# The first norm's root applied at the eviction of the mixer's projections, and six batches of roots in the tail

## The chip, the cores and the metric

The kernel runs on one core of one Trainium2 chip. The metric is device time of one execution in microseconds (us), the median of several runs. A core has TensorE (PE, matrix products), VectorE (DVE), ScalarE (ACT), GpSimd (POOL) and SyncE (SP, which issues most DMAs). Each engine takes its instructions in the order in which the program gives them and waits on semaphores.

## The reference, cut to what matters

One step of a hybrid encoder layer, for a prompt of 1024 tokens and 32 tokens of a running stream, D = 1024, everything fp32:

```python
def rms_norm(x, g):
    y = x * rsqrt(mean(x * x, -1) + EPS)
    return y * g
proj = rms_norm(x, norm_mix_g) @ w_in      # 8 projections of width 1024
lx, lg, q, k, v, rg, ga, gb = split(proj)
# RG-LRU branch: conv of width 4, two gates, a scan
xc = conv_b + sum(xp[:, j:j + L] * conv_w[j] for j in range(4))
r, i = sigmoid(xc_block @ lru_wa + ba), sigmoid(xc_block @ lru_wx + bx)
a = exp(-8 * r * softplus(-lambda)); mult = sqrt(1 - a * a)
h[t] = a[t] * h[t-1] + mult * i * xc
y_lru = (gelu(lg) * h) @ w_lru_o
# retention branch, 8 heads of 128: rotary q and k, chunkwise state, group norm
y_ret = (silu(rg) * head_group_norm(retention(rope(q), rope(k), v))) @ w_ret_o
out = x + (sigmoid(ga) * y_lru + sigmoid(gb) * y_ret) @ w_out
# then a top-1-group / top-2-expert mixture of 32 SwiGLU experts, a residual,
# and a final rms_norm of every row
```

The factor rsqrt(mean(x*x) + EPS) is one number per token, and g one per feature. So `(x * g) @ w` times the token's factor is the same projection as the norm's output times w.

## The kernel before, in words

Features lie on the partitions and tokens along the free dimension: T = 1056 tokens in CT = 3 columns of CW = 352. Every fp32 product is made of three fp32r products of a high and a low part: `w_hi`, `w_lo` for a block of 128 output features, `xn_hi`, `xn_lo` for the normalised x. A "product" is one block of 128 outputs for all tokens: 3 columns x 8 k x 3 matmuls.

`Mixer` holds two weight slots s = 0, 1, each with three PSUM banks, one per column. `Jobs` numbers the products of a slot (turn): SP loads the raw weights, POOL splits them (`split`), PE runs `column`, and an engine that empties a bank raises `tile_free[s]`, for which PE's next turn of the slot waits.

- `normalise` (L258): ACT squares x, PE sums over features with a matrix of ones, ACT takes the root, DVE the reciprocal and x * g * r per k, ACT makes `xn_hi`, DVE `xn_lo`. The first two products' columns run in between. DVE computes softplus of lambda in some 25 small steps while x lands.
- `lru` (L434), 8 blocks n: slot 0 holds the conv's input, slot 1 GELU's. ACT copies the first out of PSUM (`conv_input`, L522 to L529), applies GELU out of PSUM (L537), sigmoids (L544), exp and tanh (L551, L552), sqrt (L563). DVE runs `conv` (L576, L579), `mult` (L594 to L597) and `scan` (L604 to L615). PE's gate matmuls (L504), two per column, go between the columns of other products; their two banks `pg` are freed by the sigmoids of the column before. For blocks 0 and 1 they stand a column later than for the others.
- `merge` (L644), twice (`ml`, `mr`): u is split by ACT (L743) and DVE (L751), ACT takes the sigmoid of a gate product out of PSUM (L736), DVE multiplies it by the branch's product (L763).
- `retention` (L830), 8 heads, 7 of them in a loop: four products v, k, q, gate. ACT copies v, k and q out of PSUM and applies SiLU to the gate's (`take`, L1046; `srg` is the buffer). DVE rotates k (L1143 to L1146) and q (L1171 to L1180), accumulates the states (L1191 to L1197), masks scores (L1155), normalises and gates (L1133). PE turns tokens and features (L886, L888) and builds states (L968) in two further banks that follow one another in the fixed order of `Turns.ORDER`; ACT's `take_k_t` (L1079) empties the banks of turned k, the last of them right after the first SiLU.
- `experts`: 32 experts, PE-bound. In its tail (`last_step` of ACT, L2276 and L2290; DVE L2431 to L2442; POOL L2049) the rows of h are squared and summed, rooted in five batches (`BATCHES`), scaled and stored, and the last three experts' 96 rows each are scattered by six indirect DMAs.

The order on ACT within a block n of `lru` is what the prediction follows:

```python
for n in range(KD):
    sigmoids(n)
    decay(n)
    if n < LAST:
        conv_input(n + 1)
    act.wait_ge(m2_done, n + 1)
    act.activation(mu[:], mu[:], ACT.Sqrt).then_inc(mult_out, 1)
    if n < LAST:
        gelu(n + 1)
```

and on DVE: `mult(n)`, `conv(n + 1)`, `scan(n)`.

Of the kernel before, what the change touches and what calls it, by code (L numbers as in the profile page):

```python
# [85 lines left out]
CN_ID = 0  # L86
CN_TRI = CN_ID + P
# [4 lines left out]
CN_N = CN_SLOT + SLOTS  # L92
# [6 lines left out]
def shape_tables():  # L99
# [26 lines left out]
    cn[:, CN_ID:CN_ID + P] = np.eye(P)  # L126
# [40 lines left out]
class Mixer:  # L167

    def __init__(self, nc, ctx, R):
# [10 lines left out]
        self.spare = sb("spare", [P, T])  # L180
        self.psum = [self.bank_set(ctx, s) for s in range(2)]
# [76 lines left out]
def normalise(nc, keep, A, R, J, following):  # L258
# [6 lines left out]
    with ExitStack() as ctx:  # L265
        sb = lambda n, s, d=F32: ctx.enter_context(nc.sbuf_tensor(f"nm_{n}", s, d))
        sem = lambda n: R.spend(keep.enter_context(nc.semaphore(f"nm_{n}")))
        x = R.u.rearrange("p (c k t) -> p c k t", c=CT, k=KD)
        sq = [sb(f"square{b}", [P, KD, CW]) for b in range(2)]
        rms = [sb(f"rms{b}", [P, CW]) for b in range(2)]  # L270
        ones = sb("ones", [P, 4 * P])
        warm = sb("warm", [P, 2])
        sp_e, sp_s, sp_q, sp_a = (sb(n, [P, 8]) for n in ("sp_e", "sp_s", "sp_q", "sp_a"))
# [4 lines left out]
        sq_done, summed = sem("sq_done"), sem("summed")  # L278
        rms_done, xn_done = sem("rms_done"), sem("xn_done")
        hi_done, lo_done = sem("hi_done"), sem("lo_done")  # L280
        abs_done, exp_done = sem("abs_done"), sem("exp_done")
        lam_done, dve_step = sem("lam_done"), sem("dve_step")
        cols = lambda c: slice(c * CW, (c + 1) * CW)

    def sync(sp):
# [4 lines left out]
        sp.dma_start(R.par[:], A["par_columns"]).then_inc(par_in, 16)  # L290
        load(0)
        for s in range(2):
            J.load(sp, s, 0, following[s])
        load(1)
        load(2)
        sp.dma_start(R.const[:], A["const_small"]).then_inc(const_in, 16)
# [4 lines left out]
    def tensor(pe):  # L301
        def sums(c):
            if c == 2:
                pe.wait_ge(rms_done, 1)
            for m, ks in enumerate(PARTS[c]):
                pe.wait_ge(sq_done, PARTS_BEFORE[c] + m + 1)
                for k in range(ks.start, ks.stop):
                    mm = pe.matmul(total[c % 2][:, 0:CW], ones[:, 0:P], sq[c % 2][:, k, :],
                                   start=(k == 0), stop=(k == KD - 1))
            mm.then_inc(summed, 1)  # L310

        def column(s, c):
# [3 lines left out]
            for m, ks in enumerate(HALVES):  # L316
                pe.wait_ge(hi_done, 2 * c + m + 1)
# [3 lines left out]
            for m, ks in enumerate(HALVES):  # L321
                pe.wait_ge(lo_done, 2 * c + m + 1)
# [7 lines left out]
        sums(0)  # L330
        sums(1)
        for c in range(CT):
            for s in range(2):
                column(s, c)
                if c == 0 and s == 0:
                    sums(2)
        pe.wait_ge(const_in, 16)

    def scalar(act):
        def square(c):  # L340
            if c == 2:
                act.wait_ge(summed, 1)
            for m, ks in enumerate(PARTS[c]):
                act.wait_ge(x_in[c][m], 16)
                act.activation(sq[c % 2][:, ks, :], x[:, c, ks, :], ACT.Square).then_inc(sq_done, 1)

        def root(c):
            act.wait_ge(summed, c + 1)
# [12 lines left out]
        act.activation(sp_e[:], sp_a[:], ACT.Exp, scale=-1.0).then_inc(exp_done, 1)  # L361
        act.activation(warm[:, 1:2], R.eps[:], ACT.Sqrt)
# [4 lines left out]

        square(0)
        weights(0)
        root(0)  # L370
        weights(1)
        square(1)
        hi(0)
        root(1)
        square(2)
        hi(1)
        root(2)
        hi(2)
        act.wait_ge(par_in, 16)
        act.wait_ge(lam_done, 2)  # L380

    def vector(dve):
        dve.memset(ones[:], 1.0).then_inc(set_done, 1)
        dve.memset(R.eps[:], EPS).then_inc(set_done, 1)
        dve.memset(R.stage[:], 0.0)
        dve.wait_ge(par_in, 16)
# [3 lines left out]
        st.link(dve.tensor_scalar(sp_s[:], lam, -1.0, None, ALU.mult))  # L390
        dve.tensor_tensor(sp_a[:], sp_s[:], lam, ALU.max).then_inc(abs_done, 1)
        dve.wait_ge(exp_done, 1)
        st.link(dve.tensor_scalar(sp_q[:], sp_e[:], 2.0, None, ALU.add))
        st.link(dve.reciprocal(sp_q[:], sp_q[:]))
        st.link(dve.tensor_tensor(sp_e[:], sp_e[:], sp_q[:], ALU.mult))
        st.link(dve.tensor_tensor(sp_q[:], sp_e[:], sp_e[:], ALU.mult))
        st.link(dve.memset(sp_a[:], 1.0 / (2 * LOG_TERMS - 1)))
        for j in range(LOG_TERMS - 2, -1, -1):
            st.link(dve.tensor_tensor(sp_a[:], sp_a[:], sp_q[:], ALU.mult))
            st.link(dve.tensor_scalar(sp_a[:], sp_a[:], 1.0 / (2 * j + 1), None, ALU.add))  # L400
        st.link(dve.tensor_tensor(sp_a[:], sp_a[:], sp_e[:], ALU.mult))
        st.link(dve.tensor_scalar(sp_s[:], sp_s[:], 0.0, None, ALU.max))
        st.link(dve.scalar_tensor_tensor(out=sp_s[:], in0=sp_a[:], scalar=2.0, in1=sp_s[:],
                                         op0=ALU.mult, op1=ALU.add))
        dve.tensor_scalar(R.lam_neg[:], sp_s[:], -8.0, None, ALU.mult).then_inc(lam_done, 1)
        dve.tensor_scalar(R.lam_pos[:], sp_s[:], 8.0, None, ALU.mult).then_inc(lam_done, 1)
# [5 lines left out]

        weights(0)
        for c in range(CT):
            r = rms[c % 2]
            dve.wait_ge(rms_done, c + 1)
            st.link(dve.reciprocal(r[:], r[:]))
            for k in range(KD):
                ins = dve.scalar_tensor_tensor(out=x[:, c, k, :], in0=x[:, c, k, :],
                                               scalar=R.par[:, PR_GMIX + k:PR_GMIX + k + 1], in1=r[:],  # L420
                                               op0=ALU.mult, op1=ALU.mult)
                if k % 4 == 3:
                    ins.then_inc(xn_done, 1)
            for m, ks in enumerate(HALVES):
                dve.wait_ge(hi_done, 2 * c + m + 1)
                dve.tensor_tensor(M.xn_lo[:, ks, cols(c)], x[:, c, ks, :], M.xn_hi[:, ks, cols(c)].bitcast(F32),
                                  ALU.subtract).then_inc(lo_done, 1)
            if c == 0:
                weights(1)

    return Programs(sync, gpsimd, tensor, scalar, vector)


def lru(nc, keep, A, R, J, following):  # L434

    M = J.M
    with ExitStack() as ctx:
# [27 lines left out]
        xp_set = sem("xp_set")  # L465
        CG = XC // CT
# [51 lines left out]
    def scalar(act):  # L518
        def conv_input(n):
            if n:  # L520
                act.wait_ge(conv_step, n * CONV_STEPS)
            act.activation(xp[:, PAD + SEQ:PAD + SEQ + PAD],  # L522
                           R.par[:, PR_CACHE:PR_CACHE + 24].rearrange("p (j n) -> p j n", n=KD)[:, :, n], ACT.Copy)
            for c in range(CT):
                J.tile_ready(act, 0, n, c)
                lo, hi = c * CW, min((c + 1) * CW, SEQ)
                ins = act.activation(xp[:, PAD + lo:PAD + hi], psum[0][c][:, 0:hi - lo], ACT.Copy)
                if hi - lo < CW:
                    ins = act.activation(xp[:, PAD + S0:XP], psum[0][c][:, hi - lo:CW], ACT.Copy)  # L529
                ins.then_inc(M.tile_free[0], 1)  # L530

        def gelu(n):
            if n >= 2:
                act.wait_ge(u_done, n - 1)
            for c in range(CT):
# [11 lines left out]
        def decay(n):  # L547
            act.wait_ge(gate_free[0], n * CT + CT)
            if n >= 2:
# [4 lines left out]
        act.wait_ge(xp_set, 1)  # L554
        conv_input(0)
        gelu(0)
        for n in range(KD):
            sigmoids(n)
            decay(n)
            if n < LAST:  # L560
                conv_input(n + 1)
            act.wait_ge(m2_done, n + 1)
            act.activation(mu[:], mu[:], ACT.Sqrt).then_inc(mult_out, 1)  # L563
            if n < LAST:
                gelu(n + 1)

    def vector(dve):
# [32 lines left out]
        def scan(n):  # L600
# [12 lines left out]
            J.taken(dve, 1, n)  # L613
# [3 lines left out]
        dve.memset(xp[:], 0.0).then_inc(xp_set, 1)  # L617
        dve.wait_ge(xp_set, 1)
        conv(0)
        for n in range(KD):  # L620
            mult(n)
# [2064 lines left out]
```

## Time and profile before

| | |
|---|---|
| median of 3 runs | 1844.86 us (1843.6 to 1845.11) |
| profiled execution, its own time | 1845.6 us |
| its span in the trace | 1843.7 us |
| mean granted PE clock | 0.984 |

The page's slices (40 equal parts of the span, busy share in tenths; PEclk is the granted TensorE clock):

```profile
PE   8999999999999999999999979989999999999993
...
DVE  7565580001455445554621143367888888998886
ACT  5455460001122111221310023227878878788784
...
PEclk9999999999999999999999989989999999999997
```

A slice is 46 us. The start is in the first one, the RG-LRU blocks end in the sixth, the first merge in the tenth, retention in the twentieth, the second merge in the twenty-fourth; the experts begin in the twenty-seventh.

### The profile page before, as it was taken

How to read it: one execution, taken by the hardware profiler on the slowest of the kernel's cores; microseconds unless marked ns; L12 is line 12 of the kernel's file. 1: busy time of each engine (PE TensorE's matmuls, PEld its weight loads, DVE VectorE, ACT ScalarE, POOL GpSimd, SP SyncE). 2: the span in 40 equal slices, each digit the busy share in tenths (PEclk: the TensorE clock that was granted, in tenths of full speed). 3: DMA queues.
4: the chain of work that ended last, by engine and by line, in shares of the span. 5: the costliest groups of instructions: out<-in, count | busy, mean ns of one | idle time of the engine just before them, and what ended most of it. 6: DMA issues, size and time to landing. Idle time of an engine off the chain costs nothing. (4 is left out here: it accounts for less than half of the span.)

```text
span 1843.7 us, 25685 instructions
## 1 busy us (share of the span) xinstructions
PE 1781.3 (97%) x10105; PEld 1547.5 (84%) x10105; DVE 1063.2 (58%) x1242; ACT 780.6 (42%) x914; POOL 497.3 (27%) x286
## 2 busy tenths in 40 slices
PE   8999999999999999999999979989999999999993
PEld 6989999999999999999999978857777777777772
DVE  7565580001455445554621143367888888998886
ACT  5455460001122111221310023227878878788784
POOL 0432322223222222222233310022332332234331
PEclk9999999999999999999999989989999999999997
DMA  4111122223111111111132456558999999999993
GB/s 151 38 52 52 29 57 72 70 70 116 50 38 34 37 37 48 37 34 37 38 104 93 142 184 228 200 205 318 369 390 376 381 382 376 385 382 396 382 343 133
DMA packets 146514, 316.52 MB, mean 172 GB/s; under 512 B 11153, under 2 KB 106481, under 8 KB 121720
## 3 DMA queue, kind: packets, MB, share of 16 engines
q1 hardware_dynamic: 135896, 287.79, 42.4%
q0 software_dynamic: 10528, 27.48, 5.4%
q8 instruction: 63, 1.03, 0.2%
q14 instruction: 27, 0.22, 0.0%
HBM read 288.16 MB, written 36.47 MB: 176 GB/s over the span
## 5 line engine op out<-in xcount | busy, mean ns | idle before, releaser
L227 PE MATMUL job_ps<-xn_hi,w_hi 128*128 128x352 f32 x1488 | 494.0, 332 | 0.3 <-issue 0.3
L229 PE MATMUL job_ps<-xn_hi,w_lo 128*128 128x352 f32 x1488 | 478.3, 321 | 0.0
L228 PE MATMUL job_ps<-xn_lo,w_hi 128*128 128x352 f32 x1488 | 477.6, 321 | 0.0
L210 POOL CAST w_hi<-w_raw 128x1024 fp32r<-128x1024 f32 x78 | 85.3, 1094 | 765.5 <-issue 445.3
L227 PEld LDWEIGHTS job_ps<-xn_hi,w_hi 128*128 128x128 f32 x1488 | 279.4, 188 | 4.0 <-issue 0.7
L228 PEld LDWEIGHTS job_ps<-xn_lo,w_hi 128*128 128x128 f32 x1488 | 280.2, 188 | 2.3
L229 PEld LDWEIGHTS job_ps<-xn_hi,w_lo 128*128 128x128 f32 x1488 | 279.6, 188 | 0.0
L212 POOL TENSOR_TENSOR w_lo<-w_raw,w_hi 128x1024 fp32r<-128x1024 f32 x78 | 205.0, 2629 | 6.3
L2369 DVE TENSOR_TENSOR ex_raw_lo<-ex_raw,ex_w_hi 128x2048 fp32r<-128x2048 f32 x88 | 200.0, 2284 | 10.8 <-ACT ex_w_hi L2237 10.7
L2237 ACT ACTIVATE ex_w_hi<-ex_raw 128x2048 fp32r<-128x2048 f32 x88 | 168.8, 1918 | 52.8 <-PE ex_y L2106 23.9
L763 DVE TENSOR_TENSOR gate<-job_ps,gate 128x352 f32<-128x352 f32 x48 | 25.2, 525 | 280.0 <-PE job_ps L229 280.0
L736 ACT ACTIVATE gate<-job_ps 128x352 f32<-128x352 f32 x48 | 20.6, 463 | 276.0 <-DMA merged_lru<-gate 121.6
L2369 DVE TENSOR_TENSOR u_lo<-u,ex_w_hi 128x2048 fp32r<-128x2048 f32 x52 | 118.3, 2286 | 13.8 <-ACT ex_w_hi L2237 11.7
L2369 DVE TENSOR_TENSOR raw_more_lo<-raw_more,ex_w_hi 128x2048 fp32r<-128x2048 f32 x52 | 118.3, 2285 | 9.2 <-ACT ex_w_hi L2237 9.1
L2237 ACT ACTIVATE ex_w_hi<-u 128x2048 fp32r<-128x2048 f32 x52 | 99.5, 1917 | 35.3 <-PE ex_y L2106 14.7
L2237 ACT ACTIVATE ex_w_hi<-raw_more 128x2048 fp32r<-128x2048 f32 x52 | 99.6, 1917 | 28.6 <-PE ex_up L2106 12.3
L2104 PE MATMUL ex_gate<-ex_w_hi,ex_x_hi 128*96 128x512 f32 x260 | 103.9, 399 | 3.2 <-DVE ex_x_lo L2375 2.3
L2104 PE MATMUL ex_up<-ex_w_hi,ex_x_hi 128*96 128x512 f32 x260 | 104.3, 401 | 0.0
L2106 PE MATMUL ex_gate<-ex_w_hi,ex_x_lo 128*96 128x512 f32 x260 | 103.8, 399 | 0.0
L2106 PE MATMUL ex_up<-ex_w_hi,ex_x_lo 128*96 128x512 f32 x260 | 102.5, 394 | 0.0
L2015 POOL DMA_INDIRECT ex_rows<-xf_rows,h_row x32 | 91.5, 2859 | 36.6 <-POOL h_row L2003 23.7
L2104 PE MATMUL ex_y<-ex_w_hi,ex_h_hi 128*96 128x512 f32 x248 | 99.3, 401 | 0.0
(325 smaller groups left out, 3311.4 us busy)
## 6 DMA issues: line engine op xcount, KB each, us to landing
ex_raw<-in_w_chunks SPq DMA_DIRECT2D x88, 1024.0 KB, 10.2
u<-in_w_chunks SPq DMA_DIRECT2D x52, 1024.0 KB, 8.5
raw_more<-in_w_chunks SPq DMA_DIRECT2D x52, 1024.0 KB, 9.1
w_raw<-in_w_in SPq DMA_DIRECT2D x64, 512.0 KB, 4.1
merged_lru<-gate SPq DMA_DIRECT2D x8, 528.0 KB, 5.1
spare<-merged_lru SPq DMA_DIRECT2D x8, 528.0 KB, 5.8
merged<-gate SPq DMA_DIRECT2D x8, 528.0 KB, 4.9
w_raw<-in_w_lru_o SPq DMA_DIRECT2D x8, 512.0 KB, 4.2
```

Source lines behind the costliest of these rows:

```text
L210: pool.tensor_copy(M.w_hi[s][:], M.w_raw[s][:]).then_inc(M.hi_done[s], 1)
L212: pool.tensor_tensor(M.w_lo[s][:], M.w_raw[s][:], M.w_hi[s][:].bitcast(F32), ALU.subtract).then_inc(M.split_done[s], 1)
L227: pe.matmul(out, M.w_hi[s][:, k, :], x_hi[:, k, cols], start=(k == 0), stop=False)
L228: pe.matmul(out, M.w_hi[s][:, k, :], x_lo[:, k, cols], start=False, stop=False)
L229: mm = pe.matmul(out, M.w_lo[s][:, k, :], x_hi[:, k, cols], start=False, stop=(k == KD - 1))
L736: act.activation(sg[j % 2][:, c * CW:(c + 1) * CW], psum[s][c][:, 0:CW], ACT.Sigmoid).then_inc(M.tile_free[s], 1)
L763: dve.tensor_tensor(m[:, cols], psum[s][c][:, 0:CW], m[:, cols], ALU.mult).then_inc(M.tile_free[s], 1)
L2015: pool.indirect_dma_start(out=xe[b][0:SLOTS, :], out_offset=None, in_=xf_rows, in_offset=bass.IndirectOffsetOnAxis(ap=row[e % ROWS][:], ax ...
L2104: pe.matmul(out, a_hi, b_hi, start=first, stop=False)
L2106: return pe.matmul(out, a_lo, b_hi, start=False, stop=last)
L2237: act.activation(w_hi[n % SPLIT][:], raw[n % RAW], ACT.Copy).then_inc(hi_done, 1)
L2369: dve.tensor_tensor(w_lo[n % RAW], raw[n % RAW], w_hi[n % SPLIT][:].bitcast(F32), ALU.subtract).then_inc(lo_done, 1)
```

## The change: what it does

1. `start` takes the place of `normalise`. x * g (without the root) is split as it lands: ACT writes `xn_hi` with the weight g as scale, DVE `xn_lo` with one fused instruction per k. The squares are halved twice by DVE before PE sums them. The reciprocal root of each token is kept in `M.r` (128 partitions wide). SP loads the first weight block ahead of x.
2. Whoever needs a projection multiplies it by `M.r`: on DVE for the conv's input, GELU's input, the merge gates and the gate of retention. Their non-linear functions then run on ACT out of SBUF and in place. For q the factor is put once into the rotary tables; k gets it there and a second time, for v, by one more multiply per head.
3. Softplus of lambda moves behind the first conv.
4. The identity is a small input of its own; the other constants load in the second stage.
5. In the tail there are six batches of roots for five, two tiles' squares are taken earlier, and the third scatter to the sample rows goes ahead of the prompt's.

```diff
@@ start, scalar @@
+        weights(0)
+        hi(0)
+        weights(1)
         square(0)
...
+        hi(1)
+        square(1)
+        root(0)
+        hi(2)
+        square(2)
+        root(1)
         root(2)
@@ start, vector @@
         weights(0)
+        lo(0)
+        weights(1)
+        pairs(0)
+        lo(1)
+        pairs(1)
+        turned_round(0)
+        lo(2)
+        p.first_block(dve, 0)
+        pairs(2)
+        turned_round(1)
+        p.first_block(dve, 1)
+        turned_round(2)
+        p.first_block(dve, 2)
@@ lru, scalar @@
         def gelu(n):
-            if n >= 2:
-                act.wait_ge(u_done, n - 1)
-            for c in range(CT):
-                J.tile_ready(act, 1, n, c)
-                act.activation(gl[n % 2][:, c * CW:(c + 1) * CW], psum[1][c][:, 0:CW],
-                               ACT.Gelu_apprx_tanh).then_inc(M.tile_free[1], 1)
+            J.taken(act, 1, n)
+            act.activation(gl[n % 2][:], gl[n % 2][:], ACT.Gelu_apprx_tanh).then_inc(gelu_done, 1)
...
         gelu(0)
         for n in range(KD):
             sigmoids(n)
             decay(n)
-            if n < LAST:
-                conv_input(n + 1)
             act.wait_ge(m2_done, n + 1)
             act.activation(mu[:], mu[:], ACT.Sqrt).then_inc(mult_out, 1)
             if n < LAST:
                 gelu(n + 1)
+    def gate_input(dve, n, c):
+        if n >= 2 and c == 0:
+            dve.wait_ge(u_done, n - 1)
+        J.tile_ready(dve, 1, n, c)
+        at = slice(c * CW, (c + 1) * CW)
+        dve.tensor_tensor(gl[n % 2][:, at], psum[1][c][:, 0:CW], M.r[:, at], ALU.mult).then_inc(M.tile_free[1], 1)
@@ lru, vector @@
         conv(0)
+        softplus(dve)
         for n in range(KD):
+            if n:
+                for c in range(CT):
+                    gate_input(dve, n, c)
             mult(n)
             if n < LAST:
+                for c in range(CT):
+                    conv_input(dve, n + 1, c)
                 conv(n + 1)
             scan(n)
@@ merge, vector @@
     def vector(dve):
+        if not entry:
+            gate_input(dve, 0)
         u_lo_part(dve, before.late_k)
         for j in range(KD):
+            if j + 1 < KD:
+                gate_input(dve, j + 1)
@@ retention, scalar @@
-            take(1, h * 2 + 1, srg, ACT.Silu, lambda c: take_k_t(2) if c == 0 else None)
+            for c in range(CT):
+                J.tile_taken(act, 1, h * 2 + 1, c)
+                at = slice(c * CW, (c + 1) * CW)
+                act.activation(srg[:, at], srg[:, at], ACT.Silu).then_inc(silu_done, 1)
+                if c == 0:
+                    take_k_t(2)
@@ retention, vector: rotate (k only), then the loop behind q's rotation @@
-            ins = dve.tensor_tensor(x[:], x[:], half[:], ALU.add)
-            ins.then_inc(done, 1)
+            st.link(dve.tensor_tensor(x[:], x[:], half[:], ALU.add))
+            dve.tensor_tensor(x[:], x[:], M.r[:], ALU.mult).then_inc(done, 1)
...
             for c in range(3):
+                J.tile_ready(dve, 1, h * 2 + 1, c)
+                at = slice(c * CW, (c + 1) * CW)
+                dve.tensor_tensor(srg[:, at], psum[1][c][:, 0:CW], M.r[:, at], ALU.mult).then_inc(M.tile_free[1], 1)
                 bank, free = turns.ready(dve, kind, h, h, "kv", c)
@@ retention, vector, before the first head @@
+        for at in (TB_COS, TB_SIN):
+            dve.tensor_tensor(tb[:, at:at + T], tb[:, at:at + T], M.r[:], ALU.mult).then_inc(table_set, 1)
@@ retention, vector, last head @@
         p.next_split(dve, range(4))
+        p.next_gate(dve)
@@ experts, tail @@
-        BATCHES = ((0, 3), (3, 6), (6, NTILE + 1), (NTILE + 1, NTILE + 2), (NTILE + 2, NTILE + 3))
+        BATCHES = ((0, 2), (2, 4), (4, 7), (7, NTILE + 1), (NTILE + 1, NTILE + 2), (NTILE + 2, NTILE + 3))
...
             h_part(LAST - 1)
+            square_tile(0)
             hi(LAST - 1, 5)
+            act.activation(warm[:], R.eps[0:1, :], ACT.Sqrt)
             hi(LAST, 4)
-            act.activation(warm[:], R.eps[0:1, :], ACT.Sqrt)
+            square_tile(1)
             h_part(LAST)
             hi(LAST, 5)
```

## Rows read from the trace of the kernel before

**Rows 1.** The page, part 1 (totals) and part 5 (costliest groups; last columns busy and idle).
```profile
PE 1781.3 (97%) x10105; PEld 1547.5 (84%) x10105; DVE 1063.2 (58%) x1242; ACT 780.6 (42%) x914; POOL 497.3 (27%) x286
...
L763 DVE TENSOR_TENSOR gate<-job_ps,gate 128x352 f32<-128x352 f32 x48 | 25.2, 525 | 280.0 <-PE job_ps L229 280.0
```

**Rows 2.** Timeline of the start: start us, length us, engine, line, names, [idle before].
```profile
8.63 0.79 ACT L345 ACTIVATE nm_square<-u 128x704 f32<-128x704 f32 x1 [1.25 <-DMA u<-in_x_columns]
...
12.65 2.34 DVE L417 RECIPROCAL nm_rms<-nm_rms 128x352 f32<-128x352 f32 x1
...
15.03 4.06 DVE L419 SCALAR_TENSOR_TENSOR u<-u,par,nm_rms 128x352 f32<-128x352 f32 x8
...
19.00 3.15 DVE L426 TENSOR_TENSOR xn_lo<-u,xn_hi 128x1408 fp32r<-128x1408 f32 x2
...
51.08 0.40 PE L227 MATMUL job_ps<-xn_hi,w_hi 128*128 128x352 f32 x1 [0.28 <-issue]
```

**Rows 3.** Timeline of PE in the RG-LRU stage, gate matmuls.
```profile
121.28 1.35 PE L504 MATMUL lru_pg<-conv_out,w_gates 128*128 128x353 f32 x4
...
137.76 1.35 PE L504 MATMUL lru_pg<-conv_out,w_gates 128*128 128x353 f32 x4
...
142.79 1.35 PE L504 MATMUL lru_pg<-conv_out,w_gates 128*128 128x353 f32 x4
...
242.66 2.96 PE L504 MATMUL lru_pg<-conv_out,w_gates 128*128 128x353 f32 x8 [0.70 <-ACT r_gate L544]
```

**Rows 4.** Timeline of DVE in the RG-LRU stage.
```profile
86.07 2.29 DVE L606 TENSOR_TENSOR_SCAN hidden<-decay_a,i_gate 128x1024 f32<-128x1024 f32 x1
...
125.75 1.26 DVE L594 TENSOR_TENSOR mult<-decay_a 128x1059 f32<-128x1059 f32 x1 [9.23 <-ACT decay_a L551]
...
130.26 4.04 DVE L579 SCALAR_TENSOR_TENSOR conv_out<-conv_in,par,conv_out 128x1059 f32<-128x1059 f32 x3
...
136.50 4.35 DVE L606 TENSOR_TENSOR_SCAN hidden<-decay_a,i_gate 128x1024 f32<-128x1024 f32 x1
...
142.32 0.19 DVE L615 TENSOR_TENSOR u<-gelu_gate,hidden 128x32 f32<-128x32 f32 x1
```

**Rows 5.** Timeline of ACT in the RG-LRU stage.
```profile
124.54 1.18 ACT L551 ACTIVATE decay_a<-r_gate,lam_neg 128x1059 f32<-128x1059 f32 x1
...
134.62 1.28 ACT L544 ACT_TABLE_LOAD   x1
...
138.55 0.56 ACT L544 ACTIVATE r_gate<-lru_pg,par 128x353 f32<-128x353 f32 x1 [2.64 <-PE lru_pg L504]
```

**Rows 6.** Timeline of PE behind two gaps.
```profile
15.26 7.71 PE L308 MATMUL nm_total<-nm_square,nm_ones 128*128 128x352 f32 x16 [3.39 <-ACT nm_square L345]
...
111.17 1.43 PE L504 MATMUL lru_pg<-conv_out,w_gates 128*128 128x353 f32 x4 [2.96 <-issue]
```

**Rows 7.** Windows: stretch, busy time of each engine, granted clock PEclk, DMA share, GB/s.
```profile
20.00:22.00 2.00, 2.00 (x7) 1.21 (x6) 2.00 (x2) 0.50 (x1) 0.00 (x0) 0.81 0.36 94
```

**Rows 8.** Timeline of DVE, entry of the first merge.
```profile
261.99 12.48 DVE L751 TENSOR_TENSOR ml_u_lo<-u,ml_u_hi 128x1056 fp32r<-128x1056 f32 x8
```

**Rows 9.** Timeline of all engines, first head and one head of the retention loop.
```profile
454.82 1.25 DVE L1143 TENSOR_TENSOR ret_rotary_half<-ret_k_features,ret_tables 64x1056 f32<-64x1056 f32 x1 [12.43 <-DMA ret_state_in<-in_state_ret]
...
577.95 0.63 PE L886 MATMUL ret_turn<-const,ret_k_features 128*128 128x128 f32 x4 [0.26 <-DVE ret_k_features L1146]
...
589.41 0.34 ACT L1079 ACTIVATE ret_k_tokens<-ret_turn,ret_tables 32x128 f32<-32x128 f32 x1
...
592.34 1.05 PE L968 MATMUL ret_turn<-ret_v_tokens,ret_k_tokens 128*128 128x128 f32 x8
...
593.02 0.18 DVE L1180 TENSOR_TENSOR ret_q_features<-ret_q_features,ret_tables 128x32 f32<-128x32 f32 x1
```

**Rows 10.** Timeline of the tail, DVE and POOL.
```profile
1813.54 0.18 DVE L2438 RECIPROCAL ex_fi_rstd<-ex_fi_rms 128x3 f32<-128x3 f32 x1 [2.33 <-ACT ex_fi_rms L2290]
...
1827.95 1.27 POOL L2049 DMA_INDIRECT out<-ex_y_rows,rt_sample_row  x1 [33.91 <-DVE ex_y_rows L2442]
```

More of the change, by code:

```diff
@@ L302, in sums @@
         def sums(c):
+            pe.wait_ge(added, c + 1)
             if c == 2:
                 pe.wait_ge(rms_done, 1)
[L305 to L309, printed above, removed]
+            for k in range(2):
+                mm = pe.matmul(total[c % 2][:, 0:CW], ones[:, 0:P], sq[c % 2][:, k, :], start=(k == 0), stop=(k == 1))
             mm.then_inc(summed, 1)
@@ L329, in tensor @@
             pe.matmul(total[1][:], ones[:, 0:P], ones[:], start=True, stop=True)
-        sums(0)
-        sums(1)
         for c in range(CT):
[L333 to L336, printed above, removed]
+            column(0, c)
+            if c == 2:
+                sums(2)
+            column(1, c)
+            if c < 2:
+                sums(c)
         pe.wait_ge(const_in, 16)
@@ L389, in vector @@
         lam = R.par[:, PR_LAM:PR_LAM + 8]
[L390 to L406, printed above, removed]
+        st.link(dve.tensor_scalar(M.sp_s[:], lam, -1.0, None, ALU.mult))
+        dve.tensor_tensor(M.sp_a[:], M.sp_s[:], lam, ALU.max).then_inc(abs_done, 1)
         def weights(s):
@@ L431, in normalise, with lo @@
-    return Programs(sync, gpsimd, tensor, scalar, vector)
+        def lo(c):
+            for m, ks in enumerate(PARTS[c]):
+                dve.wait_ge(hi_done, PARTS_BEFORE[c] + m + 1)
+                for k in range(ks.start, ks.stop):
+                    ins = dve.scalar_tensor_tensor(out=M.xn_lo[:, k, cols(c)], in0=x[:, c, k, :], scalar=gain(k),
+                                                   in1=M.xn_hi[:, k, cols(c)].bitcast(F32), op0=ALU.mult, op1=ALU.subtract)
+                ins.then_inc(lo_done, 1)
@@ L565, in scalar, with first_block_begins, first_block, conv_input @@
                 gelu(n + 1)
+    def first_block_begins(dve):
+        dve.memset(xp[:], 0.0).then_inc(xp_set, 1)
+    def first_block(dve, c):
+        dve.wait_ge(M.r_done, c + 1)
+        conv_input(dve, 0, c)
+        gate_input(dve, 0, c)
+    def conv_input(dve, n, c):
+        if c == 0:
+            if n:
+                dve.wait_ge(conv_step, n * CONV_STEPS)
+                dve.wait_ge(xc_done, n)
+            else:
+                dve.wait_ge(xp_set, 1)
+            dve.tensor_copy(xp[:, PAD + SEQ:PAD + SEQ + PAD],
+                            R.par[:, PR_CACHE:PR_CACHE + 24].rearrange("p (j n) -> p j n", n=KD)[:, :, n])
+        J.tile_ready(dve, 0, n, c)
+        lo, hi, end = c * CW, min((c + 1) * CW, SEQ), (c + 1) * CW
+        ins = dve.tensor_tensor(xp[:, PAD + lo:PAD + hi], psum[0][c][:, 0:hi - lo], M.r[:, lo:hi], ALU.mult)
+        if hi < end:
+            ins = dve.tensor_tensor(xp[:, PAD + S0:XP], psum[0][c][:, hi - lo:CW], M.r[:, hi:end], ALU.mult)
+        ins.then_inc(M.tile_free[0], 1)
@@ L1306, in iota @@
         def iota(n, ts):
[L1308 removed]
+            return H.const[:, CN_IOTA:CN_IOTA + n].unsqueeze(1).broadcast_to((P, ts.stop - ts.start, n))
         st = Steps(None, step)
```

248 lines of the change are left out of this document (131 added, 117 removed).

## The prediction

> **What bounds the kernel now.** I read the page's totals first: TensorE (PE) is busy 97% of 1843.7 us, VectorE (DVE) 58%, ScalarE (ACT) 42% [rows 1]. PE takes its instructions in one order, so the time is PE's work plus every wait in that order, and a delay of any PE instruction before the tail moves the end one for one. The timelines of the changed stages then show three places where the other engines' order matters: the start, the eight RG-LRU blocks, the retention heads; the tail is the fourth. I count against the profiled execution's own 1845.6 us, 0.7 above the median of the runs shown. A difference of 0.2% (3.7 us) is about what a measurement of this kernel can tell from no change.
>
> **The start.** PE's first ordinary product begins at 51.08 [rows 2]. Before it, each third of x waits for its root, a reciprocal (2.34) and eight scalings (4.06) on DVE before it can be split. Afterwards the split doesn't wait for the root. I follow DVE, the longest chain. The first third of x lands at 8.63 [rows 2], now behind one 512 KB weight block: about 10.1 (estimate). ACT's last pair 0.8, DVE's last pair 1.1 (0.51 each, a fused instruction of 352 columns): 12.1. Second weight split 14.0; the squares on ACT end at 15.9 (four of 0.79), pair sums 2.5 (the 1408-column subtraction takes 1.57, half of 3.15, and half that again): 18.4. Then second third 4.1, its pair sums 2.5, reciprocal 2.3, third third 4.1, first block's two evictions 1.1, pair sums 2.5: 35.0. PE now waits there for the sums: 1.2, and 3.9 for the last column: 40.1 instead of 51.08. The conv of block 0 waits for two more reciprocals and the last evictions and comes some 1.1 later than PE asks. Gain 9.8, bounds 7 and 11. The logarithm's some 25 small operations move behind that conv and end before the first decay asks for them: nothing.
>
> **The RG-LRU blocks.** This is the term that decides. Times from here are offsets from PE's last gate matmuls of a block (121.28 [rows 3]).
> Before: the three multiplies of `mult` start at +4.47 and the conv's three accumulating ones at +8.98 [rows 4], one short instruction (0.86) earlier the conv itself, +8.1. The scan part ends at +21.2 (142.51). Meanwhile PE has a product and a column to do: it asks for gate matmuls (n+1, 0) at +16.48 and (n+1, 1) at +21.51 [rows 3]. For these ACT is ready: GELU of the next block has run long before, and the sigmoid's table is loaded at 134.62, before the sigmoids at 138.55 [rows 5]. DVE is idle 9.2 before the next `mult` [rows 4].
> After: ACT's order is still GELU(n+1), sigmoids(n+1), but GELU now waits for `gate_input(n+1)`, which stands on DVE behind `scan(n)`. And PE's gate matmuls (n+1, 1) reuse a bank that sigmoid (n+1, 0) must empty. So what was parallel becomes one loop: mult, conv input, conv, scan, gate input, GELU, table load, sigmoid, PE, mult.
> Its length: `conv_input` on DVE is three multiplies out of PSUM, 0.525 each [rows 1], overlapping, with a small copy 1.7. That moves conv and scan from an end of +21.2 to +22.9 with every duration kept. The scan of 1024 columns is 4.35 beside POOL's split and 2.29 in a block where none runs [rows 4]; being later it misses part of it, while the conv takes some on: I take +21.9. Gate input 1.5: +23.4. GELU over 1056 columns out of SBUF, near the 1.18 of the exponential: +24.6. The sigmoid's table load, hidden before, 1.28 [rows 5]: +25.9. First sigmoid 0.56: +26.4. PE asked at +21.51: a wait of 4.9 in each of blocks 3 to 6. Block 1 the same, 5.0. In block 2 PE asks at +20.8 (its first gates come at 111.17 after their own wait of 2.96, and the column order changes there), so 5.7. In block 7 three gate steps stand back to back, ending at 245.62, +18.2 from block 6's last gates (a block repeats after 16.48 + 2 x 5.03 = 26.54, four times from 121.28 is 227.4) [rows 3]; now the first sigmoids are at +26.4 to +27.0 and two more rounds follow: +29.4, so 11.2. Sum 5.0 + 5.7 + 4 x 4.9 + 11.2 = 41.5. Bounds: POOL beside the scan as before, 1.0 more a block, 48; everything on DVE at its fastest, 1.0 less, 34.
> The Trainium skill, "ScalarE: Activation LUTs", section "What ACT_TABLE_LOAD costs", puts a switch at about 2.66 us with its drain. Here the exponential starts right behind a load of 1.28, so the row decides; by the page the loop would be 1.4 longer, some 9 us more in all.
>
> **PE's clock.** After a 3.39 us gap PE's matmuls begin at 15.26 and sixteen of them take 7.71; the granted clock is 0.81 of full from 20 to 22, so half (1.2 GHz) until about 20.7: 5.4 us [rows 6, 7]. After a gap of 2.96 the gate matmuls take their usual time (1.43 against 1.35) [rows 3, 6], so that gap cost no clock. The new gaps of 4.9 lie beyond both. A half-rate stretch of 5.4 costs 2.7 of work, all of it between gates (n+1, 1) and (n+1, 2), which is inside the loop. I take 2.4 for each of seven gaps, 16.8; bounds 0 and 20. The Trainium skill, "TensorE: Matmul & The Clock Gate", section "HAM oscillation — how this bites in real kernels", says that a kernel whose waits recur pays the return to full rate at every one of them. The trace bears it out once in two such gaps.
>
> **Merges.** Each gate tile is multiplied on DVE (1.5) and then goes through the sigmoid, a product ahead of its use: nothing in the steady part, PE's 11.5 us product covers it. At the entry of the first one `gate_input(0)` stands before the eight subtractions that start at 261.99 and take 1.56 each [rows 8]; PE uses the sixth about when it is done. Plus 1.2 there, and 1.5 at the second merge, where it stands before the last head's gating. Bounds 0 and 2 each. If the cover were gone in the steady part it would be 1.5 for each of 14, 21.
>
> **Retention.** Two waits, both seven times. (a) The rotated k gets one more multiply of 1056 columns, 1.26 (the first of the rotation takes 1.25). PE already waits 0.26 for the rotated k at 577.95 [rows 9], so all of it lands on PE: 1.3. Beside POOL's split it could be 3.3. (b) `srg` is now filled by DVE after the q rotation, which ends at 593.20, later 594.5. Column 0's multiply 0.5, ACT's SiLU 0.6 with its signals, and only then ACT empties the last k bank (0.34, which it did at 589.41): 595.9. PE's state matmuls of column 1 need that bank; they ran at 592.34, shifted by (a) 593.6 [rows 9]. Wait 2.3. Together 3.6 by 7 = 25.2. Bounds: 1.3 by 7 = 9 if (b) is covered, 5 by 7 = 35. First head: the two tables are scaled once, DVE stands waiting for them already (12.43 for the DMA [rows 9]), so 2.6 more. I count no clock in gaps of 2.3; if it fell each time, 2 by 7 = 14.
> q's rotation, later by the same, costs nothing further: its scores are asked for some 4 us behind it.
>
> **Tail.** DVE waits 2.33 for the second root at 1813.54 [rows 10]. With smaller batches and two squares moved ahead it finds work there; against that the last weight splits come 0.9 later, since ACT squares a tile (0.9 beyond its own idle time) in between. 2.33 + 0.18 (a reciprocal that stood there) - 0.9 = 1.6. POOL's six scatters, which start at 1827.95, come that much earlier; the third sample scatter, moved up, finds its rows just ready. Gain 1.6, bounds 0 and 2.4.
>
> The constants (256 KB) load in the second stage, some 100 us before their use: nothing.
>
> **Sum.** -9.8 + 41.5 + 16.8 + 1.2 + 1.5 + 25.2 + 2.6 - 1.6 = +77.4. 1845.6 + 77.4 = 1923.0.
>
> **Rivals.**
> 1. The loop closes but PE keeps its full clock: 1923.0 - 16.8 = 1906. For it, the 2.96 gap; against it, the 3.39 one. Chance 0.22; forecast with the clock 0.52.
> 2. Half rate after retention's gaps as well (14), the first k multiply contended: 1923 + 14 + 8 (1.2 more a head) = 1945. The gaps of 2.3 are shorter than one that kept the clock. 0.10.
> 3. The loop doesn't close: gate input and GELU run in DVE's and ACT's idle time as they do now (DVE is idle 9.2 a block), and retention alone pays: 1845.6 - 9.8 + 2.7 + 27.8 - 1.6 = 1865. Against it stands the order of the code: every link is an explicit wait. 0.08.
> 4. The other side, faster: the same, and PE also finds cover in retention, since ACT's and DVE's half-idle time takes the moved work. Then the start and the tail are left: 1845.6 - 9.8 - 1.6 = 1834. It decides if the moved chain in a head stays under 0.3 and in a block under 3.5 (PE's slack: conv ready at +13, asked for at +16.5). 0.07.
> The last 0.01 is no change.
>
> **How the numbers follow.** The likeliest is 1923. Low end 1886: loop at its lower bound (34), no clock, retention at 2.5 a head, the start at its best. High end 1948: case 2 and a little. That leaves out cases 3 and 4 and the extremes. Faster by over 0.2% 0.07, within 0.01, slower 0.92.
>
> **What would show it.** PE's first ordinary product at about 40. The starts of `mult` some 33 to 34 apart instead of 26.5, with PE waiting 5 for a sigmoid before each block's second gate matmuls, and a granted clock under 1 in that stage. Heads 62.2 apart instead of 58.6, PE waiting for ACT's k tokens. The end of all PE work some 79 later. It is wrong if PE has no wait at those gate matmuls: then GELU wasn't behind the scan.

## The result, and the profile after

The changed kernel takes 1924.09 us (median of 4 runs, 1921.64 to 1928.62), the kernel before 1844.61 beside it: 1.0429 times as long, 95% interval 1.0417 to 1.0442. The profiled execution took 1921.95 with a span of 1920.1, 76.4 more than before. The forecast was 1923.0.

The page's totals, and of its slices the rows that answer to those of before (a slice is now 48 us):

```profile
PE 1792.5 (93%) x10069; PEld 1554.8 (81%) x10069; DVE 1129.4 (59%) x1389; ACT 772.5 (40%) x876; POOL 486.5 (25%) x286
...
PE   8887869999999999999999997998999999999994
...
PEclk9998989999999999999999998998999999999997
```

PE falls from 97% to 93% [rows 1], and the missing tenths stand in the first six slices; in the fourth and the sixth PEclk dips too. The view of waits says for whom PE waited (engine and line that waits, releaser: us in total, times, the longest), after the change:

```profile
PE lru_pg L505 <- ACT r_gate L528: 39.8, 7, 10.4
PE ret_turn L1019 <- ACT ret_k_tokens L1130: 14.2, 7, 2.1
PE ret_turn L937 <- DVE ret_k_features L1199: 12.4, 8, 1.6
PE op_out L1712 <- DVE op_m_lo L1807: 11.1, 1, 11.1
PE lru_pg L505 <- issue: 6.7, 3, 4.0
```

The same waits before it:

```profile
PE lru_pg L504 <- issue: 3.2, 2, 3.0
PE ret_turn L886 <- DVE ret_k_features L1146: 1.8, 7, 0.3
PE lru_pg L504 <- ACT r_gate L544: 0.7, 1, 0.7
```

The first of the five is the loop that the forecast saw in the RG-LRU blocks, the next two are its waits (b) and (a) in retention. The fourth was there (10.8). The fifth, waits of a block's first gates for the conv, was 3.2 in total.

PE's timeline (start, duration, engine, line, count, idle before), which answers to [rows 3] for blocks 2 to 4 and 7. With the loop closed, a wait of 5.5 stands before each block's second gates; from there to the third gates it is 7.50 and 7.26, where it was 5.03:

```profile
126.17 1.35 PE L505 MATMUL lru_pg<-conv_out,w_gates 128*128 128x353 f32 x4
142.65 1.35 PE L505 MATMUL lru_pg<-conv_out,w_gates 128*128 128x353 f32 x4
153.37 2.72 PE L505 MATMUL lru_pg<-conv_out,w_gates 128*128 128x353 f32 x4 [5.53 <-ACT r_gate L528]
160.87 1.35 PE L505 MATMUL lru_pg<-conv_out,w_gates 128*128 128x353 f32 x4
177.34 1.35 PE L505 MATMUL lru_pg<-conv_out,w_gates 128*128 128x353 f32 x4
188.07 2.72 PE L505 MATMUL lru_pg<-conv_out,w_gates 128*128 128x353 f32 x4 [5.54 <-ACT r_gate L528]
195.33 1.35 PE L505 MATMUL lru_pg<-conv_out,w_gates 128*128 128x353 f32 x4
...
290.98 4.58 PE L505 MATMUL lru_pg<-conv_out,w_gates 128*128 128x353 f32 x8 [10.41 <-ACT r_gate L528]
```

The loop itself, on DVE (first fence) and ACT (second), read from one `mult` to the next; it answers to [rows 4, 5]:

```profile
130.64 1.26 DVE L626 TENSOR_TENSOR mult<-decay_a 128x1059 f32<-128x1059 f32 x1 [14.19 <-ACT decay_a L537]
...
134.36 1.34 DVE L568 TENSOR_TENSOR conv_in<-job_ps,rstd 128x352 f32<-128x352 f32 x3
...
136.71 4.69 DVE L611 SCALAR_TENSOR_TENSOR conv_out<-conv_in,par,conv_out 128x1059 f32<-128x1059 f32 x3
141.32 2.34 DVE L617 COPY stage<-conv_in 128x3 f32<-128x3 f32 x1
...
145.09 2.29 DVE L638 TENSOR_TENSOR_SCAN hidden<-decay_a,i_gate 128x1024 f32<-128x1024 f32 x1
...
148.95 1.38 DVE L578 TENSOR_TENSOR gelu_gate<-job_ps,rstd 128x352 f32<-128x352 f32 x3
165.34 1.26 DVE L626 TENSOR_TENSOR mult<-decay_a 128x1059 f32<-128x1059 f32 x1 [15.00 <-ACT decay_a L537]
```

```profile
150.37 1.08 ACT L522 ACTIVATE gelu_gate<-gelu_gate 128x1056 f32<-128x1056 f32 x1 [13.57 <-DVE gelu_gate L578]
151.47 1.28 ACT L528 ACT_TABLE_LOAD   x1
152.76 0.56 ACT L528 ACTIVATE r_gate<-lru_pg,par 128x353 f32<-128x353 f32 x1
```

DVE now idles 14 to 15 us a block and ACT 13.0 to 13.6 at its longest wait: each waits for the other or for PE's next gates. `mult` starts 34.2 to 34.7 apart in blocks 3 to 6 instead of 26.5; the forecast had 33 to 34.

The ledger: each row is the difference of one and the same instruction's start (in the RG-LRU row its end) in both traces, less that of the row above. The entry of a merge is DVE's first product of an output column and its gate.

| stage | forecast | measured |
|---|---|---|
| start (first gates, 58.79 to 49.35) | -9.8 | -9.4 |
| RG-LRU (last gates' end, 245.62 to 295.56) | 41.5 + 16.8 = 58.3 | 59.4 |
| entry of the first merge (278.17 to 328.64) | +1.2 | +0.5 |
| first head (first turned k on ACT, 464.76 to 516.89) | +2.6 | +1.7 |
| retention, second merge's entry (931.25 to 1011.93) | 25.2 + 1.5 = 26.7 | 28.6 |
| second merge, experts (last matmul, 1812.72 to 1892.40) | 0 | -1.0 |
| tail (to the end of the span) | -1.6 | -3.3 |
| sum (the rows are rounded) | +77.4 | +76.4 |

### The profile page after: what moved, and what is told of

Same layout as the page of the kernel before. It is cut to its first block and busy times, and to the rows that moved or that the text cites. A ratio compares the mean times of both kernels' runs of the same rounds, so it can differ in the third digit from the quotient of the medians.

```text
span 1920.1 us, 25758 instructions
## 1 busy us (share of the span) xinstructions
PE 1792.5 (93%) x10069; PEld 1554.8 (81%) x10069; DVE 1129.4 (59%) x1389; ACT 772.5 (40%) x876; POOL 486.5 (25%) x286
## 3 DMA queue, kind: packets, MB, share of 16 engines
q8 instruction: 63, 1.03, 0.2%
## 5 line engine op out<-in xcount | busy, mean ns | idle before, releaser
L229 PE MATMUL job_ps<-xn_hi,w_hi 128*128 128x352 f32 x1488 | 500.4, 336 | 0.0
L229 PEld LDWEIGHTS job_ps<-xn_hi,w_hi 128*128 128x128 f32 x1488 | 283.8, 191 | 4.5 <-issue 1.7
L230 PEld LDWEIGHTS job_ps<-xn_lo,w_hi 128*128 128x128 f32 x1488 | 284.1, 191 | 3.2 <-issue 1.5
L773 ACT ACTIVATE gate<-gate 128x352 f32<-128x352 f32 x48 | 22.5, 497 | 257.1 <-DVE gate L796 257.0
L811 DVE TENSOR_TENSOR gate<-job_ps,gate 128x352 f32<-128x352 f32 x48 | 25.2, 524 | 144.9 <-PE job_ps L231 144.9
```

The lines of the kernel that those rows point to most:

```text
L229: pe.matmul(out, M.w_hi[s][:, k, :], x_hi[:, k, cols], start=(k == 0), stop=False)
L230: pe.matmul(out, M.w_hi[s][:, k, :], x_lo[:, k, cols], start=False, stop=False)
```

## The experiments

"Blocks" is the time from the first gates to the end of the last ones in the trace: 186.8 before, 246.2 after.

### Gate input ahead of the scan

```diff
-            if n:
-                for c in range(CT):
-                    gate_input(dve, n, c)
             mult(n)
...
                 conv(n + 1)
+                for c in range(CT):
+                    gate_input(dve, n + 1, c)
             scan(n)
```

> The changed kernel with gate_input(n+1) on VectorE moved from behind scan(n) to between conv(n+1) and scan(n). ScalarE's order is untouched: GELU(n+1) still stands ahead of the sigmoids. Theory: the 59.3 us that the RG-LRU blocks lost are the loop through scan, gate input, GELU, table load and sigmoid; with gate input ready at about 16.5 behind a block's last gates, the sigmoids are ready at 20, ahead of TensorE's 21.5, and waits and clock loss both go: mult starts 26.5 apart again, time 1924.1 - 59 = 1865, 1861 to 1870. Rival: the blocks are longer because VectorE has 3.2 us more work in each (conv input and gate input) or because ScalarE's order alone is at fault: then moving one step on VectorE changes little, time above 1900.

Measured 1879.65 (ratio to before 1.0181, 1.0164 to 1.0198): 44.4 less than the changed kernel, 15 above the expected 1865 and outside its range. Blocks took 201.0. The mechanism holds, since the waits for sigmoids fell from 39.8 in seven to 6.0 in five, but the opening was too small. ACT's GELU started at 160.25, 18.9 behind the last gates, where I had gate input ready at 16.5: a copy of three elements ahead of gate input takes 2.35 here too. PE still waits 0.23 in blocks 3 to 6, and in block 7, whose gate steps stand back to back, 5.10.

### GELU later on ScalarE

```diff
-        gelu(0)
         for n in range(KD):
             sigmoids(n)
             decay(n)
+            gelu(n)
             act.wait_ge(m2_done, n + 1)
             act.activation(mu[:], mu[:], ACT.Sqrt).then_inc(mult_out, 1)
-            if n < LAST:
-                gelu(n + 1)
```

> The changed kernel with GELU(n) on ScalarE moved from ahead of the sigmoids of its block to between tanh and the square root. VectorE's order is untouched, gate input stays behind the scan; as many table loads as before. Theory: this opens the same loop at another link, so it gives the same as the kernel with gate input moved: about 1865, 1861 to 1870. Rival: it is the position of gate input on VectorE that delays mult or frees TensorE's banks too late; then the waits stay, time above 1900.

Measured 1874.95 (1.0166, 1.0136 to 1.0195; runs from 1869.36 to 1879.76). No wait for a sigmoid is left in its trace:

```profile
133.27 1.35 PE L505 MATMUL lru_pg<-conv_out,w_gates 128*128 128x353 f32 x4
138.30 1.35 PE L505 MATMUL lru_pg<-conv_out,w_gates 128*128 128x353 f32 x4
143.33 1.35 PE L505 MATMUL lru_pg<-conv_out,w_gates 128*128 128x353 f32 x4
159.80 1.35 PE L505 MATMUL lru_pg<-conv_out,w_gates 128*128 128x353 f32 x4
```

26.53 a block, as before, with DVE's order untouched: the rivals of the two runs, which blamed gate input's place on DVE or DVE's added work, fall. Two links of one loop were cut by independent edits, and both opened it. But blocks take 194.4, 7.6 more than before; the expectation left that out, and the median lies above its range. Of the time, 49 came back. The executions are up to 10 apart; only one of them has a trace, so why is not shown, and the run with the k bank below has a likely reason.

### The gap filled

```diff
+        def unused(n, c):
+            if c == 1 and n >= 3:
+                pe.wait_ge(M.tile_free[0], (n + 1) * CT)
+                for _ in range(28):
+                    pe.matmul(M.psum[0][2][:, 0:CW], M.w_hi[0][:, 0, :], M.xn_hi[:, 0, 0:CW], start=True, stop=True)
...
-                J.product(pe, 0, n + 1, M.xn_hi, M.xn_lo, lambda c: gates(n, c))
+                J.product(pe, 0, n + 1, M.xn_hi, M.xn_lo, lambda c: (unused(n, c), gates(n, c)))
```

> The changed kernel with the loop left as it is; in blocks 3 to 6 TensorE runs 28 unused matmuls of 352 columns (0.16 us each, 4.5 us) in the gap of 5.5 us before the second gate matmuls; nothing waits for them. Theory: the column behind the gap runs at half rate because of the gap (gates 2 to gates 3 take 7.0 to 7.5 instead of 5.03), and with the gap filled they take 5.0: four times 2.0 to 2.4 less, 1924.1 - 8.8 = 1915. Rival: the column is slow for another reason (missing operands, a bank, ports): nothing changes, 1924.

Second to third gates now take 5.16, four times (151.71 to 156.87 for one), and blocks 237.9, 8.3 less where 8.8 was expected. In windows behind block 3's second gates (us, busy time and count of the five engines, PEclk, DMA share, GB/s), the changed kernel and then this one:

```profile
153.00:158.00 5.00, 4.63 (x12) 3.63 (x13) 0.00 (x0) 1.88 (x4) 0.00 (x0) 0.50 0.00 0
```

```profile
151.00:156.00 5.00, 4.29 (x23) 3.86 (x24) 0.00 (x0) 2.21 (x5) 0.00 (x0) 1.00 0.01 3
```

The granted clock is 0.50, that is 1.2 GHz, behind a gap of 5.5 and full, 2.4 GHz, behind one of 1.0, in the same place with the same operands. The gap is the cause of the slow column. The time agrees less well: 1918.76 (1.0397, 1.0380 to 1.0414) where 1915 was expected, three runs at 1918.7 to 1919.0 and the profiled one at 1912.56, 9.4 under the changed kernel's profiled one. Where the other three lost 6 us has no trace.

### The k bank emptied ahead of SiLU

```diff
+            take_k_t(2)
             for c in range(CT):
                 J.tile_taken(act, 1, h * 2 + 1, c)
                 ... ACT.Silu
-                if c == 0:
-                    take_k_t(2)
```

> The changed kernel with ScalarE emptying the last bank of turned k ahead of the gate's SiLU in retention, so not behind VectorE's q rotation. Theory: TensorE's 2.1 us wait for the k tokens goes in each of seven heads, and nothing takes its place: 1924.1 - 14.7 = 1909; heads 60.1 apart, and 58.6 + 1.4 for the wait on the rotated k is what is left. If the two heads that took 1.6 longer did so for a clock that fell behind this wait, 3 more: 1906. Rival: the wait moves to the scores or to the next product's bank, since SiLU and q's rotation stay late: less than 5 us gained.

Measured 1903.29 (1.0315, 1.0298 to 1.0332), 20.8 less, and less than either expectation (1909, or 1906 with the clock). The wait for the k tokens is gone and the other stays:

```profile
PE ret_turn L937 <- DVE ret_k_features L1198: 12.4, 8, 1.6
PE ret_turn L937 <- ACT ret_k_tokens L1130: 1.0, 1, 1.0
```

Behind the first head the heads are 59.9 apart, all six distances: 2.26 less, 15.8 over seven waits. The rest comes from the clock. In the changed kernel four of the six distances are near 62.2 and two are 63.7, one of them here:

```profile
696.97 0.63 PE L937 MATMUL ret_turn<-ident,ret_k_features 128*128 128x128 f32 x4 [1.59 <-DVE ret_k_features L1199]
760.71 0.63 PE L937 MATMUL ret_turn<-ident,ret_k_features 128*128 128x128 f32 x4 [1.59 <-DVE ret_k_features L1199]
822.87 0.63 PE L937 MATMUL ret_turn<-ident,ret_k_features 128*128 128x128 f32 x4 [1.59 <-DVE ret_k_features L1199]
```

In the traces of the five other kernels with this wait one to three of the six are long. Two by 1.6 and 15.8 make 19.0; the profiled executions differ by 18.6. The changed kernel's windows in that long head, PE's k-bank wait of 2.06 standing at 711.5 to 713.56:

```profile
708.00:713.00 5.00, 3.50 (x22) 3.21 (x21) 4.63 (x8) 0.33 (x1) 0.00 (x0) 1.00 0.27 81
713.00:718.00 5.00, 4.44 (x21) 4.47 (x22) 2.93 (x8) 0.91 (x3) 0.00 (x0) 0.68 0.00 0
718.00:723.00 5.00, 5.00 (x33) 4.66 (x32) 1.56 (x3) 0.50 (x1) 2.66 (x2) 0.98 0.00 0
```

So a gap of 2.0 to 2.1 took the clock in some heads and not in others, at 1.6 each. How many heads it hits varies from trace to trace. That this also spreads the executions of one kernel is likely and not shown, since each kernel has one trace: with the wait gone the four runs lie within 1.8, and the 6.2 between the two groups of the run with the filled gap would be four more long heads.

### Tables of their own for k

```diff
+        tk = M.gate
...
-            st.link(dve.tensor_tensor(x[:], x[:], half[:], ALU.add))
-            dve.tensor_tensor(x[:], x[:], M.r[:], ALU.mult).then_inc(done, 1)
+            dve.tensor_tensor(x[:], x[:], half[:], ALU.add).then_inc(done, 1)
...
+        for i, at in enumerate((TB_COS, TB_SIN)):
+            dve.tensor_tensor(tk[i][:], tb[:, at:at + T], M.r[:], ALU.mult).then_inc(table_set, 1)
```

> The changed kernel with rotary tables of their own for k, which hold the square of the root's factor (written once, into the merge's two gate buffers), so that the multiply of 1056 columns behind each head's k rotation goes. Theory: of TensorE's 1.5 to 1.6 us wait for the rotated k, 1.3 go in each of seven heads, and the first head pays two more table multiplies less its own k multiply, 1.3: 1924.1 - 9.1 + 1.3 = 1916. The wait for the k tokens stays 2.1, since q's rotation moves with k's. Rival: the wait for the rotated k is hidden or the k tokens' wait grows by as much: 1924, with the first head's cost 1925.

Measured 1914.64 (1.0376, 1.0360 to 1.0391), 9.5 less, the theory's 8 and a little. Five of the six distances between heads are 60.86 instead of 62.15, 1.3 less each, and one is 62.43. The first head pays with a wait of 3.5 instead of 1.3. The wait for the k tokens stayed 14.2 in total.

### The tail alone

The change's edits of `BATCHES`, the squares, `turned_round` and POOL's scatters, put into the kernel before.

> The kernel before with the edits of the tail alone: six batches of roots, two squares moved ahead, the third scatter to the sample rows moved up. The forecast had 1.6 us for them; between the two traces the distance from TensorE's last matmul to the end of the span shrinks by 3.2 us. Theory one: 1.6, so 1843.7 where the kernel before takes 1845.3. Theory two: 3.2, 1842.1. Rival: the scatters wait for stores that come no earlier, 1845.3.

Measured 1842.66 against 1845.85: ratio 0.9982, 0.9973 to 0.9991, over 11 runs. 3.2, not 1.6. DVE in the tail of the kernel before and in this one:

```profile
1809.68 0.18 DVE L2438 RECIPROCAL ex_fi_rstd<-ex_fi_rms 128x3 f32<-128x3 f32 x1 [1.03 <-ACT ex_fi_rms L2290]
```

```profile
1808.91 1.40 DVE L2432 SCALAR_TENSOR_TENSOR ex_rows<-ex_y,h_w_slot,ex_rows 96x512 f32<-96x512 f32 x2
1810.23 0.15 DVE L2439 RECIPROCAL ex_fi_rstd<-ex_fi_rms 128x2 f32<-128x2 f32 x1
1810.42 2.47 DVE L2443 SCALAR_TENSOR_TENSOR ex_raw<-ex_raw,ex_fi_rstd,ex_fi_g 32x1024 f32<-32x1024 f32 x2
```

DVE waited for two roots, 1.03 and 2.33 [rows 10], 3.4 together; now it waits for neither. POOL's first scatter goes from 1827.95 to 1825.32, 2.6 earlier, and a pause of 0.57 among the scatters is 0.30 now, so the last of them ends 2.9 earlier.

### The conv's input ahead of mult

```diff
             if n < LAST:
                 for c in range(CT):
                     conv_input(dve, n + 1, c)
-                conv(n + 1)
+            mult(n)
+            if n < LAST:
+                conv(n + 1)
```

> The kernel with the late GELU, and with conv_input(n+1) on VectorE moved from behind mult(n) to ahead of it, where VectorE is idle. In the trace of the late GELU alone the eight blocks still take 7.6 us more than before (194.4 against 186.8): TensorE waits 4.0 instead of 2.96 for conv of block 2 and 2.5 instead of 0.3 for that of block 7, with a half-rate stretch behind the first. Theory: the conv input behind mult makes every conv 1 to 2 us late, and both waits and the half-rate stretch come from that; moved ahead, 7 less than the late GELU alone: 1875 - 7 = 1868, blocks in 187.5. Rival: the conv is late because of contention or because mult starts later: no change, 1875.

Blocks 187.8, as the theory had it: the waits for the conv fell from 4.0 to 2.95 and from 2.50 to 0.30. But the time is 1871.33 (1.0137, 1.0122 to 1.0153), only 3.6 less than with the late GELU alone where 7 was expected; as the two intervals overlap, the times alone do not show a gain. A new wait of 3.7 in total for `ml_u_lo` stands at the first merge's entry. DVE reaches its subtractions too late for a PE that comes 6.6 us sooner.

### All four together

> The late GELU, the early conv input, the k bank emptied ahead of SiLU, and the tables for k, all together. Theory: what is left of the change is its gain at the start (9.4) and in the tail (3.2 by the traces), against 0.5 at the first merge, some 5 for the first head's tables and 1.5 at the second merge: 1845.3 - 12.6 + 7 = 1840, 1834 to 1844; heads 58.6 apart, blocks 26.54 apart, granted clock 0.98 or more. Rival: the four losses hide one another, so that a further wait (scores, GELU, the gate's bank) comes up once they are gone: above 1850.

Measured 1846.53 against 1845.85 (1.0008, 0.9999 to 1.0017): 6.5 above the theory and outside its range, not as far as the rival's 1850, but of its kind: no difference from before. The four losses are gone (blocks 186.3, heads 58.6), and further waits came up, at two entries, where the start's gain is lost again:

```profile
PE ret_turn L937 <- DVE ret_k_features L1197: 5.2, 8, 3.1
PE job_ps L229 <- DVE ml_u_lo L785: 3.7, 2, 2.6
```

The windows behind both (us, PE busy and count, PEclk, DMA share, GB/s):

```profile
265.00:270.00 5.00, 4.88 (x22) 0.71 0.36 105
...
465.00:470.00 5.00, 5.00 (x21) 0.57 0.36 105
```

PE's last gates end 9.8 earlier than before, the first merged column is 4.1 earlier (274.03), the first turned k 0.1 earlier (464.62), and PE's last matmul starts 1.5 later (1814.26). Only the tail's gain brings the time back to that of before.

### The entries mended

The kernel of the section before with these further edits:

```diff
+            if n < LAST:
+                gelu(n)
             act.wait_ge(m2_done, n + 1)
             act.activation(mu[:], mu[:], ACT.Sqrt).then_inc(mult_out, 1)
...
+        gelu(LAST)
...
+            else:                                    # block 7, behind mult(n)
+                for c in range(CT):
+                    gate_input(dve, n, c)
...
+                early = KD - 2 if entry else 4       # k 0 to 3 of all columns first
+                for ks in (range(early), range(early, KD)):
...
+        dve.tensor_tensor(tk[1][:], M.r[:], M.r[:], ALU.mult).then_inc(table_set, 1)
+        dve.wait_ge(table_set, 1)
         dve.wait_ge(table_in, 32)
...
             rotate(st, k_f, 1, h * 2, k_rot)
+            if kind == "first":
+                for at in (TB_COS, TB_SIN):          # q's tables, now behind k's rotation
...
```

> The kernel with all four losses mended, with three more edits where its trace shows the start's gain lost again: in block 7 gate input stands behind mult and GELU behind the root (VectorE idles 1.2 there); the first merge's first output product runs k 0 to 3 for all three columns and then 4 to 7, so that it asks later for the low parts; in retention the squared root is formed before the tables land, and q's tables are scaled behind the first k rotation. Theory: in that trace TensorE waits 1.2 and 2.6 at the first merge's entry with a half-rate stretch behind (1.9), and 3.1 for the first rotated k with another (2.2); some 2.5 and 1.9 of the first group go and 3 and 2 of the second, 9 in all less what the last low parts still cost (1.5): 1846.5 - 8 = 1838.5, and a few us faster than the kernel before. Rival: the waits are set by the DMA of the tables and by the scan of block 7, not by VectorE's order: less than 3 gained, 1844 or more, no difference from before.

Measured 1834.48 (1833.62 to 1836.02) against 1846.14: 0.9939, 0.9925 to 0.9953. It beats the kernel before by 11.7 and the changed one by 89.6 us, and is 4 better than expected. The wait for `ml_u_lo` is gone and that for the first rotated k too; what is left of the latter's line is 0.3 a head:

```profile
PE lru_pg L505 <- issue: 3.2, 2, 3.0
...
PE ret_turn L943 <- DVE ret_k_features L1203: 2.1, 7, 0.3
```

Of the 11.7, 3.2 are the tail's by its own run; the other 8.5 are by subtraction what is left of the start's 9.4. The trace agrees: PE's last matmul starts at 1804.65, 8.1 earlier than before. The edits of the two entries ran together only, so which of them removed how much is not shown.

## Why the prediction was right

The start: 9.4 of 9.8; PE's first ordinary product began at 41.18, said 40. The loop in the blocks closed as described, and each of two single edits opened it; retention's two waits came as described, and one edit removed each. The single terms:

- Waits for sigmoids, forecast 5.0, 5.7, four times 4.9 and 11.2; measured 4.42, 2.85, four times 5.5 and 10.41, 39.8 for 41.5. Block 2 was over-estimated because I held its first gates' own wait at 2.96; the conv's later input raised it to 4.04, and block 7's from 0.29 to 2.50. These 3.5 us were not in the sum. They more than made up for waits that were 1.7 smaller; two errors met, and that their signs differ is luck.
- Within the loop, the step "being later it misses part of it, while the conv takes some on: I take +21.9" was wrong in its parts. The scan fell all the way to 2.29, which gives 2.06 back, and a three-element copy rose from 0.16 to 2.34. The conv took on 0.65 (4.04 to 4.69), and the multiply ahead of the scan gave 0.69 back (1.95 to 1.26). Gate input started at +22.8 and not +21.9, hence 5.5 and not 4.9.
- Clock, forecast 16.8. In blocks 3 to 6 it is 2.5, 2.2, 2.1, 2.0 between second and third gates. Over the stage 16.8 is what is left when 39.1 more wait for sigmoids and 3.5 more for the conv are taken from 59.4; that all of it is clock is not shown. Rival 1, full clock, is refuted by PEclk 0.50 behind the gap and by the filled gap. That a gap of 2.96 kept the clock in the one trace I had was luck of that execution: after 2.95 with the conv's input early, the next gates came 6.67 later, with the entries mended 6.68, with all four edits 5.09.
- Retention, forecast 3.6 a head. (a) was 1.3, as the run with tables shows. (b) was 2.0 to 2.1, forecast 2.3; undoing it gave 2.26. I counted no clock; 3.2 came of it in the profiled execution, so rival 2 held in two heads. The entry of the second merge took some 0.8 and not 1.5 (from the last head's rotated k to it 63.15 instead of 60.30, less the 2.01 of wait (b)). Over the stage that is 28.6 for 26.7.
- The tail is the term that was mis-sized most in proportion, 1.6 for 3.2: "2.33 + 0.18 - 0.9 = 1.6". Of the 0.9 of late weight splits at most 0.3 shows (PE's last matmul at 1813.06 with the tail alone, 1812.72 before), and a first wait of 1.03 was missed.
- Experts: 1.0 came back, where PE's longest waits for `ex_x_lo` and for the gathered rows went from 2.3 and 1.5 to 1.3 and 1.0. This wasn't tried further.
- The low end, 1886, is not what its own terms give: 1923 less 7.5 for the loop, 16.8 for the clock, 7.7 for retention and 1.2 for the start is 1890. And a table load that is 1.4 longer in seven blocks would cost near 10 more, where the forecast says some 9. Nothing in the outcome hangs on either.

Rival 3, no loop, and rival 4, cover in retention, fell with the first trace.

## What to carry to other kernels

A value that moves from one engine to another keeps its old place in the second engine's program unless you move that too: the projection's scaling went to VectorE behind the scan, while GELU still stood ahead of the sigmoids on ScalarE, and two engines that were busy for some 60% and 55% of these blocks before became, with TensorE, one loop. Write down, for each moved step, what waits for it and what is queued behind the waiter. And count a gain at the start only once the entries of later stages can take it: 9.4 us earlier were worth nothing until two waits, which the kernel before does not have, were moved off as well.

## What the runs showed of the hardware

The copy of three elements lasts until GpSimd's subtraction beside it ends. In the changed kernel it runs from 141.32 to 143.66, and POOL's subtraction ends at 143.64; the second fence is the copy in the kernel before, where no subtraction runs:

```profile
139.15 1.13 POOL L212 CAST w_hi<-w_raw 128x1024 fp32r<-128x1024 f32 x1 [9.14 <-PE job_ps L231]
140.36 3.28 POOL L214 TENSOR_TENSOR w_lo<-w_raw,w_hi 128x1024 fp32r<-128x1024 f32 x1
```

```profile
134.22 0.16 DVE L585 COPY stage<-conv_in 128x3 f32<-128x3 f32 x1
```

The Trainium skill, "SBUF — State Buffer", section "SBUF: two separate sides", has VectorE's two-port operations and GpSimd lock one port pair for a whole instruction, so that the loser is blocked and not slowed; these rows agree (0.16 alone, 2.34 here). That this copy is such an operation no run here shows. A cheap operation is then not cheap where it stands.

The granted clock fell behind gaps of 2.0 to 2.1 in some heads and stayed full in others, and it fell behind 2.95 in two kernels and not in a third with the same order of work there. Each fall costs 1.6 to 2.5 us in these rows. The Trainium skill, "TensorE: Matmul & The Clock Gate", section "HAM oscillation — how this bites in real kernels", says that a kernel whose waits recur pays the return to full rate at each; the rows agree, with the limit that here not every wait of one length paid.
